# A two-block fp32 network on one core: index and selection of the sparse attention moved, convolution read from PSUM, loads and turns re-placed

## What is computed

```
# first block, layer i (xl latent, xc context; ml, mc: six modulation vectors each)
z = modulate(rmsnorm(x), m[0], m[1]) @ w_in          # q, kv, conformer and short convolution parts
y = concat(attention over context and latent keys (8 heads of 96, rope),
           silu(layernorm(depthwise_conv31(a * sigmoid(g)) + b)),
           gate * depthwise_conv3(c * h))            # each rms-normed, then @ w_o
x += m[2] * rmsnorm(y);  x += m[5] * rmsnorm(relu(h2 @ w1)**2 @ w2)
# the last layer uses only keys and values of the context
# second block, layer i
qa,ka,va,za,ba,aa,ub,zb,qc,kc,vc,zc,iq,ik,iw,gates = rms_norm(x) @ w_in
ya = gated_delta_rule(silu(causal_conv4(qa,ka,va)), chunks of 64) * silu(za)
yb = pooling(ub) * silu(zb)
score = sum_h iw[h] * relu(rope(iq[h]) . rope(ik))   # 4 index heads of 64
yc = attention(qc, kc, vc on the 128 best scores of each query, causal) * silu(zc)
x += (sum_n sigmoid(gates[n]) * (y[n] @ w_branch[n])) @ w_out
```

## Time and profile before

| what | value |
|---|---|
| median of three runs | 3147.79 us |
| time of the profiled execution | 3133.03 us |
| its span in the profile | 3131.6 us |
| mean granted TensorE clock | 0.969 of full |
| PE busy | 2916.9 us, 93% |
| DVE, ACT, POOL busy | 1416.0, 1098.3, 1337.8 us |
| DMA engines busy | 28.6% |

### The profile page before, as it was taken

One profiled execution on the slowest core, in us unless ns is written; L12 is line 12 of the kernel. 1 busy time (PEld: TensorE's weight loads), 2 busy tenths in 40 slices (PEclk: granted clock), 3 DMA queues, 4 the chain that ended last, 5 costly groups with the idle time before them and its releaser, 6 DMA issues.

```text
span 3131.6 us, 41302 instructions
## 1 busy us (share of the span) xinstructions
PE 2916.9 (93%) x16444; PEld 2399.0 (77%) x16444; DVE 1416.0 (45%) x2550; ACT 1098.3 (35%) x1843; POOL 1337.8 (43%) x948
## 2 busy tenths in 40 slices
PE   7898988999999898889999899999889999998889
PEld 6576667988888675668888788887668788887677
DVE  5457543232212485532121376437762375437752
ACT  3343444552333434443332343223333332323322
POOL 4253235774444442244444344437324344346233
PEclk9899999999999999999999899999899999999999
DMA  6731314543333322122333222112113221112122
GB/s 219 301 130 51 109 62 122 180 159 98 96 100 94 107 69 83 74 74 94 94 101 95 65 88 71 55 55 68 61 54 95 72 94 57 49 59 67 56 65 84
DMA packets 81358, 291.69 MB, mean 93 GB/s; under 512 B 9104, under 2 KB 9488, under 8 KB 80784
## 3 DMA queue, kind: packets, MB, share of 16 engines
q1 hardware_dynamic: 81168, 289.06, 28.6%
HBM read 286.93 MB, written 2.10 MB: 92 GB/s over the span
## 4 chain that ended last, share of the span: by engine, by line
PE 73%; DVE 14%; issue 5%; POOL 4%; ACT 3%; DMA 1%; SPq 1%; POOLq 0%; DVEq 0%; ACTq 0%
PE ps L585 54%; PE ps L558 4%; DVE ps L2127 4%; PE ps L726 3%; POOL t L2734 2%; DVE t L2595 2%; DVE t L2593 2%; PE ps L747 2%; PE ps L613 1%; PE ps L981 1%; PE ps L990 1%; PE ps L913 1%; PE ps L995 1%; DVE t L1966 1%; POOL t L2754 1%
## 5 line engine op out<-in xcount | busy, mean ns | idle before, releaser
L585 PE MATMUL ps<-t,t 128*128 128x512 f32 (+3 forms) x9936 | 2225.9, 382 | 54.0 <-POOL t L2734 24.1
L585 PEld LDWEIGHTS ps<-t,t 128*128 128x128 f32 x9936 | 1791.9, 190 | 405.8 <-issue 48.1
L2734 POOL TENSOR_TENSOR t<-t,t 128x1024 fp32r<-128x1024 f32 (+3 forms) x444 | 1040.7, 2348 | 1065.3 <-ACT t L1280 1031.7
L1280 ACT ACTIVATE t<-t 128x1024 fp32r<-128x1024 f32 (+3 forms) x444 | 457.4, 1034 | 933.2 <-PE ps L585 880.6
L558 PE MATMUL ps<-t,t 128*128 128x128 f32 (+2 forms) x1540 | 232.6, 289 | 99.6 <-DVE t L1949 20.2
L558 PEld LDWEIGHTS ps<-t,t 128*128 128x128 f32 (+2 forms) x1540 | 181.7, 144 | 157.4 <-issue 29.3
L2227 DVE TENSOR_TENSOR ps<-ps,t 128x512 f32<-128x512 f32 (+1 forms) x96 | 57.2, 606 | 343.4 <-ACT t L1545 343.4
L2240 DVE TENSOR_TENSOR t<-ps,t 128x512 f32<-128x512 f32 x60 | 40.9, 691 | 217.7 <-PE ps L585 217.6
L2127 DVE SCALAR_TENSOR_TENSOR ps<-t,t,ps 128x512 f32<-128x512 f32 (+1 forms) x174 | 116.1, 667 | 6.1
L2754 POOL TENSOR_TENSOR t<-t,t 128x4 f32<-128x4 f32 (+2 forms) x93 | 85.5, 919 | 73.7 <-DVE t L1915 38.7
L726 PE MATMUL ps<-t,t 96*128 96x384 f32 (+1 forms) x320 | 108.9, 464 | 3.4 <-DVE t L1993 1.5
(11 more groups left out here) (259 smaller groups left out, 2620.5 us busy)
## 6 DMA issues: line engine op xcount, KB each, us to landing
t<-in_wbig SPq DMA_DIRECT2D x412, 512.0 KB, 3.5
t<-in_wmod SPq DMA_DIRECT2D x96, 512.0 KB, 5.9
t<-in_wbig SPq DMA_DIRECT2D x16, 416.0 KB, 3.2
t<-in_wbig SPq DMA_DIRECT2D x14, 256.0 KB, 2.7
t<-in_wbig SPq DMA_DIRECT2D x8, 332.0 KB, 2.9
t<-in_wbig SPq DMA_DIRECT2D x6, 384.0 KB, 3.0
t<-in_x SPq DMA_DIRECT2D x1, 2048.0 KB, 8.1
out<-t SPq DMA_DIRECT2D x1, 2048.0 KB, 6.6
```

The costliest lines, as they stand in the source:

```text
L585: m = p.matmul(out, lhs, rhs, start=kk == 0 and n == 0, stop=kk == tiles - 1 and n == 2)
L1280: a.activation(c.hi(w), c.raw(w), ACT.Copy).then_inc(w_hi.h, w_hi.up(("cut", w)))
L2734: g.tensor_tensor(c.lo(w), c.raw(w), c.hi(w).bitcast(F32), ALU.subtract).then_inc(w_lo.h, w_lo.up(("cut", w)))
```

## The change

- **Second block, order.** The gemm sm stands first, woven with prep; qa follows with the rope of the index part beside it at rate 0.3 (POOL and DVE). In ka, after ten steps, `index_in` makes the cumulative sum of the decays and the turns of the index part: 8 turns of 128 columns for the four query heads in pairs and 8 for the keys, written on both halves of the partitions (16 matmuls instead of 20, three ACT copies instead of five). qa and va use banks 4 to 7, ka and za 0 to 3.
- **Causal convolution.** `U4`, its padding and its first tap on DVE go. ACT writes the last tap (copy with a scale) to F, and DVE's other three taps read the gemm's bank in PSUM.
- **Scores and selection.** `scores` (12 products, ACT's rectification, 12 accumulations on DVE) is woven into za at rate 1.5 after seven steps. `choose` (48 rounds) stands on DVE alone, woven at 0.5 around `pool_part` and `delta`. `select` goes, and for t = 0 the causal mask is read from a constant. `nm` in `attend` is made on DVE.
- **sparse_in.** `to_branch` of the first branch and the normed qc are woven at 0.6 into vc and zc, one after the other.
- **Branch 0.** The four multiplications stand ahead of the four additions into M.
- **Attention heads.** The two banks of a head's pair are freed separately; `put` stands one step after `finish`; `conv_tail` has a period of 8 steps, not 7. Modulation groups stand at given steps (`beside`): one at step 56 of mix l0, five in heads l0, six in heads l1. Odd groups of layer 1 have slots of their own over AH and AL, and SyncE waits for the end of sb before loading them.
- **Context keys.** Four steps of `mix("c1")` go to steps 20, 36, 56 and 56 of mix l1, with a tile of their own (`ZC`).
- **Mix.** The 0.5 of the sigmoid is folded into the convolution's weights; the gate is one operation, not two; ACT makes the first tap with the bias.
- **Rates and a row.** `project` at 0.5 and 0.45 instead of 0.4; `row_of("ml1")` stands ahead of prep ml1, not behind the first group of the mlp.

The programs of ACT, DVE and POOL have the same changes of order as PE's; where they only repeat it they are left out here.

```diff
-IN2 = {"qa": [(0, 512)], "sm": [(2048, 2056), (5128, 5452)], "ka": [(512, 1024)], "va": [(1024, 1536)],
+IN2 = {"sm": [(2048, 2056), (5128, 5452)], "qa": [(0, 512)], "ka": [(512, 1024)], "va": [(1024, 1536)],
...
+def beside(main, side, at):
+
+    for n, gap in enumerate(main, 1):
+        for _ in range(at.count(n)):
+            next(side, None)
+        yield gap
+    run(side)
+
...
-                least = {(0, 4): ("sb", "c0"), (0, 5): ("wkv", "c0"), (1, 6): ("w2", "ml0", 3, 1)}.get(u)
+                least = {(0, 4): ("sb", "c0"), (0, 5): ("wkv", "c0"), (1, 1): ("sb", "l0"), (1, 6): ("w2", "ml0", 3, 1),
+                         (1, 7): ("sb", "l1")}.get(u)
...
-        return [4 * (n if n < 4 else 2 if n in (5, 7, 9) else 0) + q for q in range(4)]
+        return [4 * (n if n < 4 else 4 if n > 12 and n % 2 else 2 if n in (5, 7, 9) else 0) + q for q in range(4)]
...
-        return None if n < 4 else divmod({4: 0, 5: 2}.get(n, n - 2 if n <= 10 else n - 1), 12)
+        return None if n < 4 or n == 13 else divmod({4: 0, 5: 2, 11: 10, 12: 11}.get(n, n - 2), 12)
...
-            Q = pair(heads, ("head", n, h), (act, ("qt", n, h)), (dve, ("ktr", n, h, 0)))
-            kept.add(c.where[("head", n, h)])
+            Q = pair(heads, ("head", n, h))
+            at = c.where[("head", n, h)]
+            free[at], free[at + 1] = ((act, ("qt", n, h)),), ((dve, ("ktr", n, h, 0)),)
+            kept.add(at)
...
-        for u in range(n_u + 4):
+        for u in range(n_u + 5):
...
-            if u >= n_u - nt + 4:
-                put(n, 0, u - 4 - n_u + nt, heads)
+            if u >= n_u - nt + 5:
+                put(n, 0, u - 5 - n_u + nt, heads)
...
+    def delta_in(i):
+
+        def stream(key):
+            return product_gemm((key, i), "FM", (c.AH, c.AL), 512, 512, 8, prepared(f"d{i}"), lambda b: (
+                (dve, ("za", i, b) if key == "za" else ("c4", i, key, b)),),
+                banks=(4, 5, 6, 7) if key in ("qa", "va") else (0, 1, 2, 3))
+
+        yield from stream("qa")
+        ka = stream("ka")
+        for _ in range(10):
+            next(ka)
+            yield
+        index_in(i)
+        yield from ka
+        yield from stream("va")
+        side[:] = [4, 5, 6, 7]
+        yield from weave(stream("za"), scores(i), 1.5, 7.0)
+
+    def index_in(i):
+
+        B = c.BK[7]
+        c.where[("gc", i)] = 7
+        opened(7, ((dve, ("gc", i)),))
+        P.wait_ge(dve, ("gg", i))
+        p.matmul(B[:, 0:16], c.con("ut"), c.GG[:, :, :].rearrange("p a b -> p (a b)"), start=True,
+                 stop=True).then_inc(product.h, product.up(("gc", i)))
+        P.wait_ge(dve, ("ir", i, 3))
+        for n in range(3):
+            c.where[("ix", i, n)] = 4 + n
+            opened(4 + n, ((act, ("ix", i, n)),))
+            B = c.bank(("ix", i, n))
+            if n < 2:
+                turns([B[:, 128 * t:128 * t + 128] for t in range(4)],
+                      [c.SM[:, t, 8 + 128 * n:136 + 128 * n] for t in range(4)], ("ix", i, n))
+            else:
+                for t in range(4):
+                    for d in range(2):
+                        m = p.matmul(B[64 * d:64 * d + 64, 128 * t:128 * t + 128], c.SM[:, t, 264:328], ident,
+                                     start=True, stop=True)
+                m.then_inc(turned.h, turned.up(("ix", i, n)))
+
+    def scores(i):
+
+        for t in range(1, 4):
+            nk, cs = 128 * (t + 1), slice(128 * t, 128 * t + 128)
+            for h in range(4):
+                B = bank(side, ("ds", i, t, h), (dve, ("acc", i, t, h)))
+                P.wait_ge(act, ("ix", i, 2))
+                half = slice(64 * (h % 2), 64 * (h % 2) + 64)
+                p.matmul(B[:, 0:nk], c.IQ[half, h // 2, cs], c.IK[half, 0:nk], start=True, stop=True).then_inc(
+                    product.h, product.up(("ds", i, t, h)))
+                yield
...
-        yield from weave(delta_in(i, ("qa",)), first, 0.5)
-        yield from product_gemm(("sm", i), "TM", (c.AH, c.AL), 512, 332, 8, ready, lambda b: ((act, ("sm", i, b)),))
-        yield from delta_in(i, ("ka", "va", "za"))
+        yield from weave(product_gemm(("sm", i), "TM", (c.AH, c.AL), 512, 332, 8, ready,
+                                      lambda b: ((act, ("sm", i, b)),)), first, 0.5)
+        yield from delta_in(i)
         main[:] = [0, 1, 2, 3]
...
-    run(weave(project("c0"), both(rest, g, 4), 0.4))
+    run(weave(project("c0"), both(rest, g, 4), 0.5))
...
-    run(weave(mix("l0"), g, 0.5))
-    rest = onward(weave(heads("l0"), mods(1, 0, 6, [6, 7]), 0.22), 4 * NH + 2)
+    run(beside(weave(mix("l0"), g, 0.5), mods(1, 0, 1, [2, 6]), (56,)))
+    rest = onward(beside(heads("l0"), mods(1, 1, 6, [6, 7]), (4, 5, 12, 13, 20)), 4 * NH + 2)
...
-    run(weave(project("l0"), both(rest, g, 4), 0.4))
+    run(weave(project("l0"), both(rest, g, 4), 0.45))
...
-    g = onward(prep("l1"), 2)
-    next(keys)
-    onward(g, 2)
-    next(keys)
-    next(g)
-    run(keys)
-    run(weave(mix("l1"), g, 0.5))
-    rest = onward(weave(heads("l1"), mods(1, 6, 12, [6, 7]), 0.22), 4 * NH + 2)
+    g = onward(prep("l1"), 5)
+    run(beside(weave(mix("l1"), g, 0.5), keys, (20, 36, 56, 56)))
+    rest = onward(beside(heads("l1"), mods(1, 6, 12, [6, 7]), (4, 5, 12, 13, 20, 21)), 4 * NH + 2)
     row_of("l1", 1, 0, 0)
     next(rest)
     run(weave(project("l1"), rest, 0.4))
+    row_of("ml1", 1, 1, 0)
     g = onward(prep("ml1"), 5)
     run(weave(mlp("ml1", iter(()), 0.0), g, 0.5))
...
+                a.activation(c.bank(("cvo", n, k))[:, 0:T], c.U[:, k, 0:T], ACT.Identity, scale=W[:, k, 0:1],
+                             bias=c.c1("conf_dw_b", i)[:, k:k + 1]).then_inc(act.h, act.up(("cv", n, k)))
...
+            a.activation(c.F[n][:, b, :], c.bank(((key, i), b)), ACT.Copy, scale=w).then_inc(
+                act.h, act.up(("u4", i, key, b)))
...
-        yield from weave(product_gemm(("vc", i), 4, 8, vv), normed(i, "qc", c.TMS[1]), 0.75)
+        work = chain(iter((0,) * 4), normed(i, "qc", c.TMS[1]))
+        yield from weave(product_gemm(("vc", i), 4, 8, vv), work, 0.6, finish=False)
         turn_heads(i, "kc", c.KT2)
-        yield from product_gemm(("zc", i), 4, 8, half_silu("zc", i, c.SZ))
+        yield from weave(product_gemm(("zc", i), 4, 8, half_silu("zc", i, c.SZ)), work, 0.6)
...
-            v.tensor_scalar(G, G, 0.5, 0.5, ALU.mult, ALU.add).then_inc(dve.h, dve.up(("cg", n, k)))
-            V.wait_ge(dve, ("cg", n, k))
-            v.tensor_tensor(U, U, G, ALU.mult).then_inc(dve.h, dve.up(("cu", n, k)))
+            v.scalar_tensor_tensor(U, G, 1.0, U, ALU.add, ALU.mult).then_inc(dve.h, dve.up(("cu", n, k)))
...
-                V.wait_ge(dve, ("brx", i, n, h, b))
-                v.tensor_tensor(m, m, GT[:, b, :], ALU.add).then_inc(dve.h, dve.up(("m", i, n, 4 * h + b)))
+                if b == 3:
+                    V.wait_ge(dve, ("brx", i, n, h, b))
+                    for k in range(4):
+                        m = c.M[:, 4 * h + k, :]
+                        v.tensor_tensor(m, m, GT[:, k, :], ALU.add).then_inc(dve.h, dve.up(("m", i, n, 4 * h + k)))
...
-                v.tensor_scalar(f, c.U4[:, b, 0:512], w[:, 0:1], None, ALU.mult).then_inc(dve.h, dve.up())
                 for k in range(1, 4):
+                    v.scalar_tensor_tensor(f[:, k:512], B[:, 0:512 - k], w[:, 3 - k:4 - k], f[:, k:512], ALU.mult,
+                                           ALU.add).then_inc(dve.h, dve.up(("c4", i, key, b)))
                     V.wait_ge(dve, dve.n)
-                    v.scalar_tensor_tensor(f, c.U4[:, b, k:k + 512], w[:, k:k + 1], f, ALU.mult, ALU.add).then_inc(
-                        dve.h, dve.up(("c4", i, key, b)))
...
+    def choose(i):
+
+        m8 = c.st2[:, 40:48]
+        for t in range(1, 4):
+            SC, cs = c.SEL[t][:, :], slice(128 * t, 128 * t + 128)
+            V.wait_ge(dve, ("acc", i, t, 3))
+            v.tensor_tensor(c.SEL[t][:, cs], c.SEL[t][:, cs], c.con("tri"), ALU.min).then_inc(dve.h, dve.up(("tri", i, t)))
+            V.wait_ge(dve, ("tri", i, t))
+            for n in range(16):
+                if n:
+                    V.wait_ge(dve, ("chosen", i, t))
+                v.max(out=m8, in_=SC).then_inc(dve.h, dve.up())
+                V.wait_ge(dve, dve.n)
+                v.match_replace(out=SC, in_to_replace=m8, in_values=SC, imm_value=MARK).then_inc(
+                    dve.h, dve.up(("chosen", i, t)))
+                yield
+            V.wait_ge(dve, ("chosen", i, t))
+            v.tensor_scalar(SC, SC, -3.2e38, -BIG, ALU.is_gt, ALU.mult).then_inc(dve.h, dve.up(("bias", i, t)))
 
     def attend(i, t):
...
+            V.wait_ge(dve, ("mx", q))
+            v.tensor_scalar(nm, mx, -SM2, None, ALU.mult).then_inc(dve.h, dve.up(("nm", q)))
...
-        yield from weave(pool_part(i), delta(i), 0.48)
+        yield from weave(weave(pool_part(i), delta(i), 0.48), choose(i), 0.5)
         yield from sparse_in(i)
```

(4 more changed lines are left out.)

398 lines of the change are left out of this document (173 added, 225 removed).

## The result

The changed kernel takes 3022.99 us in the median of four runs (3021.49 to 3036.70); the kernel before took 3144.05 in the same comparison. The ratio is 0.962, with a 95% interval of 0.9583 to 0.9658. The direction was right; the forecast was half of the gain that came.

A forecast was written before the change was run, and what follows sets the result against it. PE was taken as the bound (busy 2916.9 of 3131.6 us), so only its idle time and low clock could be won. Two layers' -37 and -23.5 elsewhere gave -60.5: 3072.5 profiled, 3087 median; range 3045 to 3132.

The forecast's parts named there:

- I take half: Attention heads: half the waits for put evictions and turned q go (-10), half the tail's (-6); together -16, bounds 0 and -31.
- The clock term: Time won from PE's low granted clock behind waits: 3 us a layer in the sparse stretch, 1.7 for the index turns.
- I keep 5 us of idle for the attention chain: Sparse stretch: of 15.9 us idle, 5 stay for logits, exponent, turn and product in order; -11 idle, -3 clock per layer.
- The share given to `nm`: Sparse attention: moving `nm` from POOL to DVE ends a wait behind 2.35 us weight cuts; counted inside the -14 per layer.
- the -2.5: Mix, ahead of q: a modulation group's 64 matmuls fill some 2 us of PE's up to 4.5 us wait for L2143.
- Selection in the delta stretch: Selection steps on DVE delay delta operations and PE behind them: +4 us per layer, bounds 0 and +60; DVE at 205 of 282.
- Scores in za: Score matmuls woven into za make PE wait if DVE leaves banks full: +2.5 us per layer, bounds 0 and +8.
- Index: Index turns and rope: wait for L2564 goes, -8.5 per layer; bounds -9 and -3, the latter if normed qc is late.
- (a): More goes: delta-stretch and score costs nil, head waits go whole, sparse stretch keeps nothing; 3051 us, chance 0.15.
- (b): Half is given back: a quarter of the selection lands on PE's path, scores cost 8 a layer; 3120 us, chance 0.20.
- (c): Idle time has a cause that stays, such as POOL weight cuts (L2734), and reappears there; 3147 us, chance 0.08.
- (d): Slower: selection steps in the delta stretch precede operations PE waits for, all 60 us a layer exposed; 3199 us, chance 0.10.

The follow-up runs named there:

- all three parts: Changed kernel with selection rounds back beside the sparse attention, negated maximum on POOL and each addition behind its multiplication, undone together: 3059.79 us.
- the first experiment: The changed kernel timed again with no edit: 3022.57 us, ratio 0.9632 to the kernel before.
- all four parts undone: Changed kernel with modulation groups woven at 0.22, a head's two banks freed as one, `put` in the step of `finish`, tail period seven: 3063.06 us.

## Why the prediction was half right

**The steps that failed.** Two terms of the sum carry the miss: "I take half" of the head waits, where nearly all went (-18.5 forecast for the head stages, -40 measured), and the sparse stretch, where 5 us of idle and a third of the clock loss were kept and almost nothing stayed (-14 forecast, -22 measured, in each layer). These two are 38 us; the profiled execution came out 36 below the 3072.5 of the sum, since smaller terms went both ways. The rest of the 60 us lies in the clock of the single executions (last section).

**The reading of what bounds the kernel held.** PE was the bound, and the gain was idle time and clock: 71 us of idle and 41 of busy time, some 5 of them work, between the profiled executions of 3133.0 and 3021.0 us. Of the 60.5 forecast some 51 were idle time and 9 clock.

**The clock term was mis-sized.** The sum took 3 us a layer for it in the sparse stretch, from three rows behind three waits, 1.7 for the index turns, and nothing in the heads: 9 in all. PE's busy time fell by 24 us in the one profiled execution of the changed kernel and by 41 in the other, some 5 of each being work. The row of the window had a better number: 1 - 0.94 over 138.8 us is 8.3 us lost, and after it 1 - 0.99 over 107.9 is 1.1. Three rows show three places; the mean clock of the stretch shows all. In the heads it would have helped less: 0.96 over 202.5 us is 8.1 us lost, and 0.97 over 179.5 after it is still 5.4. That the clock rises where waits go is read from such windows (0.95 with the rounds back, 0.94 with all three parts, against 0.99 and 1.00), and it does not follow idle time place by place: with the groups woven the head stage of l0 idles 3.8 us more than in the first experiment, at a clock of 1.00 instead of 0.98.

**The sparse stretch: -14 predicted, -22 measured** (30.9 less the 8.9 of the score matmuls that moved). Besides the clock, the step "I keep 5 us of idle for the attention chain" failed: 1.8 remained. The attention chain is long, but gemm matmuls stand between its steps and cover it once DVE's queue is short; with the rounds back in the queue 11.2 us of idle return. The share given to `nm` failed as well: back on POOL it costs 0.2 and 1.4 us a stretch, once the rounds are gone.

**The heads: -16 and -2.5 predicted, 40 measured.** The step that failed is "I take half". The waits named were the right ones (L2084, L1365, L2034, L2143) and nearly all went, from 41.2 us of the four to some 6 (for the lines of PE named in the earlier trace rows). There was no row behind the half. The bound of -31 was nearer. The mechanism of the -2.5 was wrong: the wait for L2143 was to be filled by a modulation group ahead of q, and it stays away when no group stands there (2.5 of 10.1 us with all four parts undone). What took it away is among the mix's small changes, which the sum had in a -1 for all. And none of the four parts is the cause alone: groups, `put` and period bring 7 to 9 us of idle each, and the prediction priced the period only as part of the tail.

**Selection in the delta stretch: +4 predicted, +2.5 to +4 measured.** The step and its reason held; DVE is at 190 us, not 205. Its room is smaller than its result suggests, as the doubled rounds show.

**Scores in za: +2.5 predicted, 0 measured.** PE is busy 85.90 of 85.9 us in that window. The late weight cut that the convolution from PSUM was to remove is in it: its 2.5 us of idle are gone, as said, and no tap takes over 0.752 us. No run undoes that part alone.

**Index: -8.5 predicted, -4 measured.** The step into the sparse part is 6.0 us shorter and the turns in ka take 2.2. The risk named with its lower bound came, which was also one of the signs of being wrong: the last turns wait 5.33 us for the normed qc. The sum left out that the keys on both halves make the score products 2.2 us cheaper.

**Small ones.** The start of l1 is 5.8 us shorter, but the keys' matmuls stand in the mix now; the wait by `residual` of ml1 is 1.8 us shorter with the row in it. Both are as the sum had them or less.

**Rivals.** (a), more goes, was the case that came, and its 3051 was still 28 too slow, for the clock term was missing in it too. Its -8 for a sparse stretch that keeps nothing is also less than the 5 us a layer that the forecast kept. (b), (c) and (d) did not happen: PE's waits for the weight cuts fell from 24.1 to 18.1 us; (d) became visible only with the rounds' cost doubled. Index, convolution, keys and rates were not undone by any run; what is said of them rests on the lengths of their stages.

## What to carry to other kernels

Price a stall with the clock behind it: idle time plus (1 - mean granted clock) x length of the whole stretch bounds what can leave with its waits. In the sparse stretch nearly all of both left, in the heads the idle time and only part of the clock loss. When several side streams share one in-order queue, undo them together as well as alone; here four parts gave 24 us of idle apart and 29 together (30 and 40.5 in the times). Undoing them also tells which wait was not theirs: the one for the short convolution's tap stayed away. Work moved under another stage is nearly free up to a point and then not (51 us of DVE cost 2.5, the next 51 cost 17), so measure the doubled cost before adding more.

## What was not expected of the hardware

Two executions of one kernel with equal idle time (142.3 and 143.9 us) differed by 15.7 us, PE's busy time by 17.3, at mean granted clocks of 0.976 and 0.983. So a profiled execution may be longer or shorter than the median: the kernel before was profiled at 3133.0, 11 below its median in this comparison, the changed one at 3036.7, 14 above. Of the 121 us, 25 lay in that and could be read from no trace. A sum made against one profiled execution has this error in it from the start.
